# Decode value pages issued from ScalarE's DMA queue, two behind each of its key copies, in one step of a hybrid decoder layer

## The chip, the cores and the metric

The kernel runs on one core of a Trainium2 chip. The metric is the device time of one launch in microseconds (us). TensorE, VectorE, ScalarE and GpSimd (PE, DVE, ACT, POOL in the profile) compute; SyncE (SP) issues most DMAs. DMAs can be issued from SyncE, ScalarE and GpSimd.

## The reference

One inference step of a one-layer trunk, for a prompt of 512 tokens and for 8 sequences that decode 4 tokens each over a past of 2048 tokens. The decode side, cut to what matters here (page_table has 16 pages of 128 tokens per sequence):

```python
kv_past = cache_kv[page_table, l]                      # 8 sequences x 16 pages x 128 rows x (k, v) x 10 heads x 64
k_all = jnp.concatenate([kv_past[:, :, 0, ...], k_new], axis=1)
v_all = jnp.concatenate([kv_past[:, :, 1, ...], v_new], axis=1)
o_sb  = stick_breaking_attention(q_sb, k_sb_all, v_sb_all, q_pos, k_pos)      # 4 heads
o_fox = forgetting_attention(q_fox, k_fox_all, v_fox_all, cum_q, cum, q_pos, k_pos)  # 6 heads
# three dilated groups (2 heads each) over window buffers cache_dil1..3
# then: gated merge, output projection, norm, top-2 of 16 experts, norm
```

Everything is float32. Each page holds for keys, and again for values, 128 rows of 640 floats (320 KB).

## The kernel before

It runs in stages: modulation and input projection, prompt attention, the decode loop, gated merge and output projection, routing and experts, final norm. The order on each engine is written out by hand, with semaphores between the engines; there is no scheduler.

The decode loop goes over 8 sequences. On TensorE, `read_keys` does one sequence: it turns (transposes) 16 key pages and two groups of window tiles, `turn_keys(i, b0, p)` for p = 0 to 17, five transposes a page (L1032). After pages 5, 9, 13 and at the end it scores four pages at once (`score_keys`), and after pages 7, 11, 15 and at the end it turns the score rows (`turn_scores`, L1069). Between the pages it also works on the sequence before: `column_max`, `sticks`, `sums`, and from page 13 on `weigh_values`, which multiplies the 16 value pages of the previous sequence in six steps, each of which raises `v_used`. So the values of a sequence are needed about one sequence later than its keys. The first sequence runs with nothing to weigh.

Turned key pages lie in two PSUM banks, by the parity of the page. `keys_out` copies them to `kT5`: even pages on VectorE, odd pages on ScalarE (L653). A page can be turned once the page two before it has been copied out; the copies of a group of four wait for the scores of the group before. The fifth tile of each page goes to a third bank, which VectorE copies once per four pages (L1976); page 4 and so on wait for that. ScalarE's function for a sequence is `copy_out`: for each odd p the key copy; after the copies of 5, 9 and 13 the score row copy (`rows_out`, L1495), on which `turn_scores` waits; after the copies of 1, 9 and 11 the exponentials and logarithms of the previous sequence.

Key pages land in `kring`, four slots; page p may be issued when page p - 4 has been turned (semaphore `kT_mm`). Value pages land in `vpast[0]` (in `arena`, even sequences) or `vpast[1]` (in `wring`, odd ones), 16 slots each, free when the sequence two before has been weighed. Before the change SyncE issues all of it, in `sequence(i, b0)`: key pages 0 to 3, then, except in the first sequence, value pages 0 to 11 (`early`), then key pages 4 to 15, with the three window loads (1.1 MB) behind key page 8 and one value page behind each of the key pages 12 to 15. In the first sequence a value page stands behind each key page. The page's number is read from `ptab` into a register (`value_load`) and then used as an address; an odd value page reuses the register of its key page where it can. The loops run over pairs of sequences, on SyncE (2, 3), on TensorE and ScalarE (1, 2).

## Time and profile before

| | us |
|---|---|
| time, median of 3 runs | 1674.58 (1674.17 to 1683.5) |
| span of the profiled execution | 1678.0 |
| of it the decode loop, from 561 to 957 us | 396 |
| TensorE busy (7180 matmuls) | 1355.9 |
| VectorE, ScalarE, GpSimd busy | 437.0, 361.0, 164.3 |
| waits of TensorE's page turns for a key page, in the loop | 25.8, in 14 waits |

The profile is of one execution. A line of the timeline gives start, duration, engine, line of the kernel, operation and operands; in brackets the time that the engine sat idle before it, and whose work ended that. "arena<-in_cache_kv" is a page load to the key ring or to the even value buffer, "wring<-in_cache_kv" one to the odd value buffer. PEclk is the share of TensorE's full clock that was granted. The chain of work is followed back from the last instruction: each step names what released the next; a DMA's duration there runs from its issue to its landing.

### The profile page before, as it was taken

Reading aid. Unit: us, or ns where it says so; the run is one execution under the profiler, and the core shown is the slowest. Engines: PE = TensorE matmul, PEld = TensorE weight load, DVE = VectorE, ACT = ScalarE, POOL = GpSimd, SP = SyncE. Lnnn points to the kernel's source line nnn. Section 1 sums busy time; section 2 is a strip of 40 time slices with the busy share of each in tenths; the row PEclk is TensorE's granted clock in tenths of the full one; section 3 lists DMA queues with packets and bytes.
Section 4 is the critical chain, followed back from the end, with each engine's and each line's share of the span. In section 5 each row is a group of like instructions: output and inputs, shape, how many; then the busy total and the mean of one; then the engine's idle time right before and its main releaser. Section 6 shows DMA issues by size and latency. Waiting matters only on the chain.

```text
span 1678.0 us, 20728 instructions
## 1 busy us (share of the span) xinstructions
PE 1355.9 (81%) x7180; PEld 896.7 (53%) x7180; DVE 437.0 (26%) x1205; ACT 361.0 (22%) x626; POOL 164.3 (10%) x226
## 2 busy tenths in 40 slices
PE   4699997457897578878877599999992699999956
PEld 2478785333455435545545388888771344444424
DVE  3100002454343234443444201111114111111124
ACT  2200111872222122222322100000012111111104
POOL 0000000401224000000000000000002111211100
PEclk9799998777557688999989799999996799999987
DMA  8522430395000587877786422111004899999821
GB/s 319 209 100 101 159 132 1 125 327 172 1 0 1 215 299 255 253 246 255 230 260 223 148 94 85 51 50 53 0 1 119 271 327 321 306 318 315 286 107 53
DMA packets 143862, 284.74 MB, mean 170 GB/s; under 512 B 15870, under 2 KB 66759, under 8 KB 142864
## 3 DMA queue, kind: packets, MB, share of 16 engines
q1 hardware_dynamic: 133888, 260.04, 46.8%
q0 software_dynamic: 9280, 21.59, 3.6%
q10 hardware_dynamic: 624, 2.23, 0.3%
q8 instruction: 37, 0.61, 0.2%
q14 instruction: 33, 0.27, 0.0%
HBM read 270.68 MB, written 43.24 MB: 187 GB/s over the span
## 4 chain that ended last, share of the span: by engine, by line
PE 66%; DMA 8%; issue 6%; ACT 6%; DVE 6%; SPq 4%; POOL 2%; another core or an unknown queue 1%; DVEq 0%; POOLq 0%; ACTq 0%
PE psum L764 59%; PE psum L1032 3%; DMA arena<-in_cache_kv 3%; ACT L1345 3%; DMA wring<-in_w_mod 2%; SPq L499 2%; PE psum L962 2%; SPq L495 2%; POOL wring L688 2%; DVE arena L1609 1%; ACT wring L1345 1%; ACT hT L1345 1%; DVE arena L2151 1%; DMA arena<-expert_out_rows 1%; PE psum L1069 1%
## 5 line engine op out<-in xcount | busy, mean ns | idle before, releaser
L764 PE MATMUL psum<-hT,wring 128*128 128x272 f32 x1536 | 361.2, 396 | 9.7 <-ACT hT L1345 9.7
L764 PEld LDWEIGHTS psum<-hT,wring 128*128 128x128 f32 x1536 | 294.6, 192 | 74.0 <-issue 13.6
L764 PE MATMUL psum<-arena 128*8 128x128 f32 (+6 forms) x1488 | 252.2, 372 | 15.1 <-DVE arena L1609 12.6
L764 PE MATMUL psum<-wring,arena 128*8 128x128 f32 (+3 forms) x1232 | 234.5, 460 | 31.4 <-DVE arena L2151 16.6
L764 PEld LDWEIGHTS psum<-arena 128*8 128x8 f32 (+5 forms) x1488 | 133.2, 136 | 109.2 <-issue 83.8
L764 PEld LDWEIGHTS psum<-wring,arena 128*8 128x8 f32 (+3 forms) x1232 | 99.6, 130 | 141.1 <-issue 126.1
L1032 PE MATMUL psum<-small,arena 128*128 128x128 f32 x712 | 118.1, 315 | 48.9 <-DMA arena<-in_cache_kv 25.8
L764 PE MATMUL psum<-arena,wring 128*32 128x512 f32 (+1 forms) x640 | 137.6, 569 | 2.3 <-DVE arena L1609 2.3
L1032 PEld LDWEIGHTS psum<-small,arena 128*128 128x128 f32 x712 | 91.1, 160 | 80.6 <-issue 42.1
L1345 ACT ACTIVATE arena<-psum 128x544 f32<-128x544 f32 (+1 forms) x48 | 24.2, 503 | 401.7 <-PE psum L764 401.7
L1609 DVE TENSOR_TENSOR arena<-arena,psum 128x544 f32<-128x544 f32 (+8 forms) x79 | 32.2, 431 | 217.1 <-ACT arena L1345 201.7
L764 PEld LDWEIGHTS psum<-arena,wring 128*32 128x32 f32 (+1 forms) x640 | 63.5, 147 | 46.4 <-issue 36.6
L653 ACT COPY arena<-psum 128x512 f32<-128x512 f32 x64 | 37.3, 583 | 210.5 <-PE psum L1032 98.0
L653 DVE COPY arena<-psum 128x512 f32<-128x512 f32 x64 | 44.3, 692 | 137.6 <-PE psum L764 76.7
L1345 ACT ACT_TABLE_LOAD x61 | 78.3, 1283 | 1.9 <-PEq L2229 0.9
L764 PE MATMUL psum<-arena,small 128*128 128x256 f32 (+8 forms) x142 | 39.1, 402 | 34.9 <-DVE arena L1609 29.7
L688 POOL TENSOR_SCALAR wring<-wring,arena 128x384 f32<-128x384 f32 (+6 forms) x32 | 45.6, 1425 | 184.0 <-DVE arena L1824 184.0
L1650 DVE TENSOR_REDUCE modT<-psum 128x36 f32<-128x144 f32 (+1 forms) x12 | 3.7, 308 | 218.4 <-PE psum L803 218.4
L1617 DVE SCALAR_TENSOR_TENSOR arena<-psum,arena 128x256 f32<-128x256 f32 x24 | 11.6, 484 | 187.9 <-ACT arena L1345 187.9
L764 PEld LDWEIGHTS psum<-arena,small 128*128 128x128 f32 (+2 forms) x142 | 25.9, 218 | 57.4 <-issue 30.2
L764 PE MATMUL psum<-oT,arena 128*128 128x272 f32 x192 | 49.9, 404 | 6.8 <-DMA wring<-in_w_in 6.8
L1264 PE MATMUL psum<-small,arena 128*128 128x128 f32 x192 | 25.8, 279 | 34.0 <-DMA arena<-expert_in_rows,arena 34.0
(223 smaller groups left out, 1108.1 us busy)
## 6 DMA issues: line engine op xcount, KB each, us to landing
arena<-in_cache_kv SPq DMA_DIRECT2D x192, 320.0 KB, 3.7
wring<-in_w SPq DMA_DIRECT2D x48, 1024.0 KB, 11.3
wring<-in_w_mod SPq DMA_DIRECT2D x12, 2048.0 KB, 11.9
wring<-in_w_in SPq DMA_DIRECT2D x12, 2048.0 KB, 11.5
arena<-in_w SPq DMA_DIRECT2D x24, 1024.0 KB, 5.1
wring<-in_cache_kv SPq DMA_DIRECT2D x64, 320.0 KB, 4.1
out_dil_sample<-in_cache_dil SPq DMA_DIRECT2D x8, 2044.0 KB, 37.6
arena<-in_cache_dil SPq DMA_DIRECT2D x16, 512.0 KB, 5.5
```

The lines of the kernel that those rows point to most:

```text
L495: ids[p] = sp.value_load(ptab[0:1, bass.ds(b * PAGES + p, 1)], min_val=0, max_val=159)
L499: sp.dma_start(dst, pg[:, :, kv].rearrange("o k h d -> k (o h d)")).then_inc(sem(done), 16)
L653: copy(kT5[:, 0:4, c:c + 128], src.rearrange("p (j n) -> p j n", j=4)).then_inc(sem("kT_evA" if p % 2 else "kT_evD"), 1)
L688: nc.gpsimd.tensor_scalar(s, s, rowst[:, 3, n % 3:n % 3 + 1], None, ALU.mult).then_inc(sem("nrm"), 1)
L764: return T.matmul(out, lhsT, rhs, start=start, stop=stop, **k)
L962: last = T.transpose(banks[2 + tg % 2][:, 128 * (b - b0):128 * (b - b0) + 128], sc_sb[:, n % 3, 128 * b:128 * b + 128], ident)
L1032: last = T.transpose(d, a, ident)
L1069: last = T.transpose(banks[5][:, 128 * b:128 * b + 128], src[:, 128 * b:128 * b + 128], ident)
L1264: last = T.transpose(banks[k // 4][:, 128 * (k % 4):128 * (k % 4) + 128], xrow[:, slot, 128 * k:128 * k + 128], ident)
L1345: return A.activation(out, in_, fn, **k)
L1609: return V.tensor_tensor(out, a, b, op)
L2151: V.tensor_copy(xg[:, slot, 512:1024], banks[1]).then_inc(sem("xg_evD"), 1)
```

## The change

SyncE no longer issues value pages in the decode loop. ScalarE issues them in `copy_out`, pages p - 1 and p right behind the key copy of each odd p up to 15, into the same buffers, with the same semaphores. Before each of them, from the third sequence of its numbering on, it waits until the sequence two before has been weighed (all six steps). Each value page reads its number from `ptab` into a register of its own. SyncE keeps the key pages and the windows, whose wait for `v_used` at page 8 stays. Computation on TensorE, VectorE and GpSimd is unchanged.

```diff
-                def values(p):
-
-                    free = ((sem("v_used"), i * 2 * PV_STEPS + (PV_STEPS * (b0 - 2) + min(p // 2, PV_STEPS - 1) + 1)),) \
-                        if b0 >= 2 and p % 2 == 0 else ()
-                    page(p, 1, vpast[par][:, p, :], f"ld_v{par}", free)
...
-                early = 12 if b0 else 0
                 for p in range(PAGES):
...
                     if p == 8 and b0 >= 2:
-
-                        free += ((sem("v_used"), i * 2 * PV_STEPS + PV_STEPS * (b0 - 1)),)
+                        sp.wait_ge(sem("v_used"), i * 2 * PV_STEPS + PV_STEPS * (b0 - 1))
                     page(p, 0, kring[:, p % 4, :], f"ld_k{p % 4}", free)
-                    if p == 3:
-                        for v in range(early):
-                            values(v)
                     if p == 8:
                         windows()
-                    if p >= early:
-                        values(p)
...
+            def values(i, b0, p):
+
+                par = b0 % 2
+                if b0 >= 2:
+                    act.wait_ge(sem("v_used"), i * 2 * PV_STEPS + PV_STEPS * (b0 - 1))
+                page = act.value_load(ptab[0:1, bass.ds((i * 2 + b0) * PAGES + p, 1)], min_val=0, max_val=159)
+                rows = I["cache_kv"][bass.ds(page, 1), 0][:, :, 1].rearrange("o k h d -> k (o h d)")
+                act.dma_start(vpast[par][:, p, :], rows).then_inc(sem(f"ld_v{par}"), 16)
+
             def copy_out(i, b0, before):
                 steps = {1: (stick_logs,), 9: (softmax_weights,), 11: (stick_weights,)} if before else {}
                 for p in range(1, 18, 2):
                     keys_out(act, i, b0, p, A.copy)
+                    if p < PAGES:
+                        values(i, b0, p - 1)
+                        values(i, b0, p)
                     if p in (5, 9, 13):
                         rows_out(i, b0, (p - 5) // 4)
```

SyncE, in the loop, an even sequence: key page 3 and what follows it. Before, value pages 0 and 1 come next (ISA is a register or wait instruction, TENSOR_LOAD the load of a page number):

```order
L499 ISA [waits kT_mm]
L499 DMA arena<-in_cache_kv 128x640
L495 TENSOR_LOAD ptab
L495 ISA x2
L498 ISA
L499 ISA [waits v_used]
L499 DMA arena<-in_cache_kv 128x640
L499 ISA
L499 DMA arena<-in_cache_kv 128x640
L495 TENSOR_LOAD ptab
```

The same place after the change: key page 3, then key page 4, which waits only for page 0 to be turned:

```order
L499 ISA [waits kT_mm]
L499 DMA arena<-in_cache_kv 128x640
L495 ISA
L495 TENSOR_LOAD ptab
L495 ISA x2
L498 REGISTER_ALU
L499 ISA [waits kT_mm]
L499 DMA arena<-in_cache_kv 128x640
```

Twelve value DMAs and their register loads have gone from between these two key pages.

ScalarE, in the loop, an odd sequence: the key copy of page 5, the score row copy, and the wait of the next key copy, before:

```order
L649 REGISTER_ALU [waits kT_mm]
L653 COPY arena<-psum 128x4x128 [waits qk_mm]
L1492 ISA [waits qk_mm]
L1495 COPY wring<-psum 128x512 [waits sT_mm]
L647 REGISTER_ALU
L653 COPY arena<-psum 128x4x128 [waits qk_mm,kT_mm]
```

The same place after; between the two copies stand the issues of value pages 4 and 5 (line numbers shifted by the edit):

```order
L636 REGISTER_ALU [waits kT_mm]
L640 COPY arena<-psum 128x4x128 [waits qk_mm]
L1489 ISA
L1489 TENSOR_LOAD ptab
L1489 ISA x2
L1491 ISA
L1491 DMA wring<-in_cache_kv 128x640
L1489 ISA
L1489 TENSOR_LOAD ptab
L1489 ISA x2
L1491 ISA
L1491 DMA wring<-in_cache_kv 128x640
L1479 ISA [waits qk_mm]
L1482 COPY wring<-psum 128x512 [waits sT_mm]
```

Two page number loads and two DMA issues now stand ahead of the score row copy.

## Rows read from the trace of the kernel before

**Rows 1.** Busy time by sequence: stretch length, engines, clock, DMA share, GB/s; sequences 0, 1, 2, 4, 6.
```profile
564.50:606.70 42.20, 29.60 (x161) 16.76 (x162) 10.61 (x26) 8.30 (x15) 0.00 (x0) 0.77 0.94 333
606.70:655.20 48.50, 37.76 (x375) 23.93 (x374) 18.40 (x57) 12.77 (x23) 3.44 (x5) 0.89 0.84 275
655.20:700.00 44.80, 36.79 (x376) 23.88 (x375) 18.92 (x60) 12.77 (x23) 3.43 (x5) 0.92 0.83 262
...
745.80:795.20 49.40, 37.01 (x376) 23.09 (x375) 18.90 (x60) 12.77 (x23) 3.44 (x5) 0.90 0.80 259
...
840.00:888.00 48.00, 37.24 (x375) 23.74 (x375) 19.10 (x60) 12.77 (x23) 3.43 (x5) 0.89 0.85 268
```

**Rows 2.** Waits in the decode loop: us in total, times, longest.
```profile
PE psum L1032 <- DMA arena<-in_cache_kv: 25.8, 14, 5.4
```

**Rows 3.** Chain of work, sequence 4: start us, us, what.
```profile
740.21 0.33 SPq L499
...
741.39 0.33 SPq L499
...
750.26 3.46 DMA arena<-in_cache_kv
...
757.96 6.74 DMA arena<-in_cache_kv
```

**Rows 4.** TensorE's timeline, sequence 4: start us, us, what, idle before in brackets.
```profile
753.76 2.40 PE L1032 MATMUL psum<-small,arena 128*128 128x128 f32 x10 [2.60 <-DMA arena<-in_cache_kv]
...
764.83 1.30 PE L1032 MATMUL psum<-small,arena 128*128 128x128 f32 x5 [1.79 <-DMA arena<-in_cache_kv]
```

**Rows 5.** TensorE's timeline, sequence 2.
```profile
661.65 1.97 PE L1032 MATMUL psum<-small,arena 128*128 128x128 f32 x10 [1.08 <-DVE arena L1976]
...
668.90 0.60 PE L1069 MATMUL psum<-small,wring 128*128 128x128 f32 x4
...
671.10 0.74 PE L1032 MATMUL psum<-small,arena 128*128 128x128 f32 x5 [0.42 <-DMA arena<-in_cache_kv]
...
678.11 0.60 PE L1069 MATMUL psum<-small,wring 128*128 128x128 f32 x4
```

**Rows 6.** Chain of work, sequence 2.
```profile
665.80 5.16 DMA arena<-in_cache_kv
```

**Rows 7.** TensorE's timeline, sequence 0.
```profile
585.12 1.30 PE L1032 MATMUL psum<-small,arena 128*128 128x128 f32 x5 [2.99 <-DMA arena<-in_cache_kv]
...
592.01 0.60 PE L1069 MATMUL psum<-small,wring 128*128 128x128 f32 x4
```

**Rows 8.** Busy time before page 9 of sequence 3, behind it in sequence 4.
```profile
715.70:717.00 1.30, 0.00 (x0) 0.00 (x0) 0.00 (x0) 0.00 (x0) 0.00 (x0) 1.00 1.01 374
717.00:720.50 3.50, 2.57 (x15) 0.91 (x15) 0.80 (x2) 0.80 (x2) 0.00 (x0) 1.00 0.91 286
764.60:767.90 3.30, 3.07 (x14) 1.45 (x15) 0.00 (x0) 0.00 (x0) 0.00 (x0) 0.50 0.78 253
```

**Rows 9.** ScalarE's timeline, sequences 0 and 2.
```profile
590.58 0.59 ACT L1495 COPY wring<-psum 128x512 f32<-128x512 f32 x1
...
666.52 0.58 ACT L653 COPY arena<-psum 128x512 f32<-128x512 f32 x1 [5.65 <-PE psum L764]
667.00 0.59 ACT L1495 COPY wring<-psum 128x512 f32<-128x512 f32 x1
...
674.23 0.59 ACT L1495 COPY wring<-psum 128x512 f32<-128x512 f32 x1
```

**Rows 10.** DMA queues, expert stage: packets, MB, share; 1346:1347.5, then 1338:1340 us.
```profile
q0 software_dynamic: 116, 0.42, 69.5%
q1 hardware_dynamic: 165, 0.20, 36.7%
...
q1 hardware_dynamic: 685, 0.70, 109.3%
```

## The prediction

> **What bounds the kernel now.** I read the page's busy shares first, then the busy time by sequence of the decode loop, the waits inside it, the chain of work, and last the timelines of TensorE and ScalarE over single sequences. The loop runs from 561 to 957 us of a 1678.0 us span, eight sequences of 42.2 to 49.4 us each, and TensorE works 37 to 38 us of each of the later ones shown [rows 1]. It is the engine that sets the pace, in the order turn a key page, score, turn scores, weigh the previous sequence. Key pages cost it waiting time: 25.8 us in 14 waits [rows 2]. The reader should see that the sequences are of two kinds. Sequence 2 took 44.8 us; sequences 1, 4 and 6 took 48.5, 49.4 and 48.0 [rows 1].
>
> Sequence 4 shows why. SyncE issues the twelve early value pages 1.18 us apart, and only behind the last of them key page 4, at 750.26; TensorE, which had turned page 0 long before, waits 2.60 us for it, until 753.76 [rows 3, 4]. Without that hold the same spot costs 1.08 us, for a VectorE copy, as in sequence 2 [rows 5]. The second spot is page 9. Its key page stands in SyncE's queue behind the three window loads, lands 5.16 us after issue in sequence 2 and 6.74 us after it in sequence 4, and TensorE waits 0.42 and 1.79 us [rows 3 to 6].
>
> **What the change does, part by part.** Profile and runs differ: the profiled span is 1678.0, the median of the runs 1674.6. I make the sum on the span and take 3.4 off at the end.
>
> (1) Values leave SyncE. Key page 4 is then issued as soon as page 0 has been turned. Sequences 1, 4 and 6 become like sequence 2: 48.5 + 49.4 + 48.0 - 3 x 44.8 = 11.5 us less [rows 1]. The least this can be is the wait alone, three times 2.60 - 1.08, 4.5 us; the rest of 11.5 is the TensorE clock, which fell to half in the long waits. I take 11.5, since whole sequences without the hold are there to compare.
>
> (2) Sequence 0. Nine value pages, 2.9 MB, stand in SyncE's queue ahead of key page 9, and TensorE waits 2.99 us for it, until 585.12 [rows 7]. At 374 GB/s [rows 8] 2.9 MB are 7.9 us. The gain is then limited by TensorE's own work before page 9, most of whose first pages also wait for keys; by hand it can be there some 5.1 us earlier, at least 3.0. Part (3) gives back 1.7 of that. I take 3.4 (1.3 to 5.1).
>
> (3) ScalarE gets 16 issues per sequence, two behind each odd key copy. It has no id to reuse, so each is a register load and a DMA, for which the nearest row is SyncE's 1.18 us from one early value page to the next [rows 3]: 2.4 us a pair, on ScalarE's sequencer, while its copy of 0.58 us runs. What is queued behind: the score row copy, then the next key copy. After page 5 the copy starts at 666.52 and the score row copy at 667.00 [rows 9]; it would start at 668.9 and end at 669.5. TensorE turns those scores at 668.90 [rows 5], so it starts 0.7 us late, and page 8 behind it 0.3 us late; then comes page 9, which waits for its key anyway, so nothing of it shows. After page 9 the row copy moves from 674.23 to 676.1 and ends at 676.7, before TensorE wants it at 678.11 [rows 5, 9]. So in sequences 1 to 7 the issues cost nothing as long as a pair stays under about 2.9 us; above that each us of a pair is lost about twice per sequence. Sequence 0 has no weighing to cover them: the row copy at 590.58 moves to 592.5, ends at 593.1, and TensorE wanted to turn at 592.01 [rows 7, 9]: 0.9 us, and about as much once more, the 1.7 above. The wait for v_used in front of each value is already met when page 1 is turned: TensorE did the last weighing before it.
>
> (4) Values now travel while keys are awaited. Before, no value was in flight when key page 9 was; now pages 4 and 5 are issued at about 667.3 and 668.5, between the issue of key page 9 (665.80) and its landing (670.96) [rows 6, 9]. A page is 0.33 MB, at 374 GB/s 0.88 us [rows 8]. What two queues do to each other is seen in the expert stage: SyncE's queue moved 0.70 MB in 2 us alone, and 0.20 MB in 1.5 us while POOL's queue moved 0.42 MB [rows 10], that is 350 against 133 GB/s. So values are not served behind the keys but beside them. Bounds: nothing, if the second queue only fills holes; 2.0 us if both pages and a rest of pages 2 and 3 go first. I take 1.4 us later, for sequences 1 to 7: 9.8 us. The Trainium skill, "DMA: Bandwidth & Descriptors", section "Issuing engines are not separate DMA queues", says that DMAs of all issuing engines share the 16 DMA engines and interleave, and that a second issuer only saves sequencer time. By that rule alone the change would win no bandwidth and the values would land among the keys; the rows of the expert stage agree.
>
> (5) The clock. TensorE then idles about 1.5 us before page 9. In sequence 4 it idled 1.79 us and ran at half clock from there (0.50); after an idle 1.30 us in sequence 3 it stayed at 1.00 [rows 4, 8]. At half clock a page takes 1.30 against 0.74 us, and the 3.07 us of TensorE's work in that stretch would have been 1.7: 1.3 us more [rows 4, 5, 8]. I count it for three of seven sequences, 3.9 us (0 to 9.3).
>
> Sum: 1678.0 - 11.5 - 3.4 + 9.8 + 3.9 = 1676.8 on the span, less 3.4 is **1673 us** for the median. Two effects of about 15 us each cancel.
>
> **Rivals.** (B) *The values fill holes only.* Key page 9 lands as before, no clock falls: 1678.0 - 14.9 - 3.4 = 1660. For it: over the whole of sequences 1, 2, 4 and 6 the DMA engines moved 259 to 275 GB/s, below 374 [rows 1, 8]. Against it: the stretch before page 9 is the fullest of all. 0.2. (C) *Key page 9 is late by the full 2.0 us and the clock falls in each of seven sequences*: 14.0 + 9.3 instead of 13.7, so 1683, slower than before. It decides once TensorE's idle time before page 9 passes 1.8 us in every sequence. For it: queues served in turn [rows 10]. 0.18. (D) *ScalarE becomes the bound.* If its register load waits for the copy ahead, or the two issuers wait for one another, a pair may cost 4 us: turning scores late by 1.3, page 13 by 1.2 in each of seven sequences, three times 1.6 in sequence 0, 23 us more, 1696. Decides at a pair above 2.9 us. The trace has no register load on ScalarE, so only SyncE's price speaks against it. 0.1. That the hold isn't taken away is excluded by the order of SyncE's instructions.
>
> **How the numbers follow.** The forecast (effects cancel, 1667 to 1681) has 0.5; B 0.2; C 0.18; D 0.1; other 0.02. The range 1657 to 1692 takes in B and C and the near half of D. Within 1% (16.7 us, about what a measurement can tell) lie the forecast, most of C and most of B: 0.68. Faster by more needs B with more than 11.5 from part (1) or more from sequence 0: 0.14. Slower by more is D or C with dearer issues: 0.18.
>
> **What would show it.** SyncE: key page 4 issued within 0.3 us of page 0's last turn in every sequence. TensorE: waits at page 4 of about 1.1 us, on VectorE, everywhere; sequences 1, 4, 6 no longer than 2. Page 9: key landing 6 to 7 us after issue and TensorE idle 1.2 to 2 us, on a DMA; if it is 0.4, B holds. ScalarE: first to second DMA issue of a pair 1.2 us; at 2 us D holds, with TensorE's waits for ScalarE's score row copy. Sequence 0 near 39 us. The prediction is wrong if key pages other than 9 are waited for in the steady sequences, or if the half-clock stretches come elsewhere.

## The result and the profile after

The changed kernel takes 1683.41 us (median of 20 runs, 1677.31 to 1694.37) against 1675.77 us for the kernel before in the same session (20 runs, 1668.72 to 1686.44): ratio 1.0046, 95% interval 1.0028 to 1.0065. A second session gave 1683.0 against 1677.21 us, ratio 1.0024 (0.9999 to 1.0049), one of its ten executions of the changed kernel left out of the ratio because it fell in a slower state (1702.78 us). The forecast was 1673 us, a gain of 0.1%; the kernel lost 0.2 to 0.5%. The time lies in the range, within 1% of before as the forecast had it, and where rival C put it, but it moved the other way, and the balance of the forecast's terms was wrong. Each kernel was profiled twice: the spans are 1678.0 and 1673.6 us before, 1691.0 and 1682.1 us after. The rows below are of the first profile of after, an execution that took 1692.96 us, 9.6 us above the median, so they overstate the difference.

All of the difference is in the decode loop. Its busy time, for the whole loop and for sequences 0, 1, 2, 4, 5, 6, and seq 7 with the tail (columns as in [rows 1]):

```profile
563.30:977.30 414.00, 310.68 (x2985) 196.69 (x2985) 153.48 (x480) 104.70 (x185) 26.92 (x39) 0.85 0.69 240
563.30:604.90 41.60, 28.81 (x161) 16.64 (x162) 10.97 (x26) 8.31 (x15) 0.00 (x0) 0.85 0.86 303
604.90:651.20 46.30, 37.57 (x376) 23.84 (x374) 18.39 (x57) 12.84 (x23) 3.44 (x5) 0.89 0.73 254
651.20:696.50 45.30, 35.09 (x375) 22.54 (x374) 19.01 (x60) 12.85 (x23) 3.43 (x5) 0.96 0.74 260
...
743.10:794.30 51.20, 36.82 (x375) 23.96 (x374) 20.23 (x68) 12.97 (x23) 3.43 (x5) 0.90 0.66 229
794.30:845.50 51.20, 40.57 (x374) 25.78 (x375) 18.24 (x52) 12.96 (x23) 3.44 (x5) 0.84 0.68 230
845.50:896.20 50.70, 38.95 (x375) 24.33 (x376) 19.18 (x60) 12.97 (x23) 3.43 (x5) 0.87 0.67 232
896.20:977.40 81.20, 55.44 (x587) 35.79 (x586) 28.28 (x97) 18.83 (x32) 6.32 (x9) 0.73 0.58 199
```

The same query over the loop of the kernel before, first profile:

```profile
564.50:963.50 399.00, 300.67 (x2984) 191.39 (x2984) 151.66 (x480) 103.56 (x185) 26.94 (x39) 0.88 0.76 248
```

TensorE runs the same matmuls and is busy 10 us longer (310.68 against 300.67), and its mean granted share of the clock fell from 0.88 to 0.85. In the clock's records TensorE spent 120.4 us of the loop at the lower level (1.2 of 2.4 GHz), against 95.2 us before. Its waits moved. TensorE's waits in the loop (us in total, times, longest):

```profile
PE psum L1019 <- DMA arena<-in_cache_kv: 20.0, 9, 5.3
PE psum L1056 <- ACT wring L1482: 16.3, 18, 1.7
...
PE psum L1019 <- issue: 4.7, 2, 3.9
```

The waits for key pages are fewer than in [rows 2], 9 against 14, but they sit at another place. TensorE's timeline before and after page 9 of sequence 5:

```profile
800.84 2.66 PE L1019 MATMUL psum<-small,arena 128*128 128x128 f32 x10 [1.08 <-DVE arena L1975]
...
808.99 0.63 PE L1056 MATMUL psum<-small,wring 128*128 128x128 f32 x4 [0.65 <-ACT wring L1482]
809.46 0.71 PE L1019 MATMUL psum<-small,arena 128*128 128x128 f32 x5
813.14 0.74 PE L1019 MATMUL psum<-small,arena 128*128 128x128 f32 x5 [2.98 <-DMA arena<-in_cache_kv]
813.80 3.01 PE L751 MATMUL psum<-arena,wring 128*32 128x512 f32 x10
818.44 3.19 PE L751 MATMUL psum<-arena,small 128*128 128x256 f32 x6 [1.63 <-DVE arena L1608]
821.57 2.40 PE L1019 MATMUL psum<-small,arena 128*128 128x128 f32 x10
```

Page 4 is no longer held: its wait is the 1.08 us for VectorE that [rows 5] has in sequence 2. Page 9 is held for 2.98 us, where [rows 4, 5] have 1.79 and 0.42. Stretches of the same profile, the wait of sequence 5 first, and then the three at half clock that begin late in the waits at page 9 of sequences 5, 6 and 7, or just behind:

```profile
811.00:814.46 3.46, 1.32 (x13) 0.80 (x14) 0.00 (x0) 0.00 (x0) 0.00 (x0) 1.00 1.02 403
814.46:824.70 10.24, 8.61 (x26) 4.70 (x21) 2.79 (x7) 3.81 (x7) 0.00 (x0) 0.50 0.55 174
862.25:869.07 6.82, 4.85 (x15) 1.49 (x15) 0.12 (x1) 0.12 (x1) 0.00 (x0) 0.50 0.76 288
913.45:927.10 13.65, 11.19 (x35) 6.03 (x36) 2.79 (x7) 3.81 (x7) 0.00 (x0) 0.50 0.58 194
```

While TensorE waits, the DMA engines are full (403 GB/s). Right behind it they move 174 GB/s, and TensorE works at half clock for 10.24, 6.82 and 13.65 us, where [rows 8] showed a stretch of 3.3 us behind the wait of sequence 4. Behind the waits of sequences 2 and 4 (1.08 and 1.85 us) there is no such stretch. At page 4 there is one of 3.4 or 6.8 us in each of sequences 1 to 7, in both kernels and all four profiles, although the wait there is 1.08 us in most of them. The bytes that stood in front of key page 9 would have had room a few us later. They also had room earlier: at the end of sequence 4 the queues show, after and then before,

```profile
DMA packets 35, 0.06 MB, mean 7 GB/s; under 512 B 28, under 2 KB 28, under 8 KB 32
```

```profile
DMA packets 1270, 2.86 MB, mean 308 GB/s; under 512 B 153, under 2 KB 153, under 8 KB 1270
```

(786.0 to 794.3 us of after, 786.0 to 795.3 us of before). Before, value pages filled the end of the sequence; after, the DMA engines are nearly idle there.

### The profile page after: what moved, and what is told of

Its sections match the earlier page's. It is cut to its first block, busy times and chain, and to the rows that moved or that the text cites. A ratio compares the mean times of both kernels' runs of the same rounds, so it can differ in the third digit from the quotient of the medians.

```text
span 1691.0 us, 20932 instructions
## 1 busy us (share of the span) xinstructions
PE 1364.5 (81%) x7180; PEld 900.2 (53%) x7180; DVE 438.3 (26%) x1205; ACT 362.2 (21%) x627; POOL 164.4 (10%) x226
## 3 DMA queue, kind: packets, MB, share of 16 engines
q1 hardware_dynamic: 115456, 218.09, 38.4%
## 4 chain that ended last, share of the span: by engine, by line
PE 70%; DMA 6%; DVE 6%; ACT 6%; issue 6%; POOL 2%; another core or an unknown queue 2%; ACTq 1%; SPq 1%; DVEq 0%; POOLq 0%
PE psum L751 60%; PE psum L1019 4%; ACT L1332 2%; DMA wring<-in_w_mod 2%; PE psum L1056 2%; POOL wring L675 1%; PE psum L949 1%; DMA arena<-in_cache_kv 1%; DVE arena L1608 1%; ACT hT L1332 1%; DVE arena L2150 1%; DMA arena<-expert_out_rows 1%; ACT wring L1332 1%; ACTq L1491 1%
## 5 line engine op out<-in xcount | busy, mean ns | idle before, releaser
L751 PEld LDWEIGHTS psum<-hT,wring 128*128 128x128 f32 x1536 | 293.0, 191 | 74.1 <-issue 13.7
L751 PE MATMUL psum<-arena 128*8 128x128 f32 (+6 forms) x1488 | 251.8, 371 | 13.2 <-DVE arena L1608 10.8
L751 PE MATMUL psum<-arena,wring 128*32 128x512 f32 (+1 forms) x640 | 141.3, 582 | 2.3 <-DVE arena L1608 2.3
L751 PE MATMUL psum<-arena,small 128*128 128x256 f32 (+8 forms) x142 | 43.6, 438 | 35.8 <-DVE arena L1608 30.5
## 6 DMA issues: line engine op xcount, KB each, us to landing
wring<-in_w SPq DMA_DIRECT2D x48, 1024.0 KB, 11.5
```

Source lines behind the costliest of these rows:

```text
L751: return T.matmul(out, lhsT, rhs, start=start, stop=stop, **k)
```

## The experiments

Two theories. K: the value bytes beside the keys make key page 9 late, and the waits lower the clock. I: the issues on ScalarE's own order cost the time, by what stands behind them.

**Which of the two.** In the first, the score row copy goes ahead of the value issues, in the second a value load brings a tenth of its bytes, in the third SyncE issues all, at nearly the same points (12 to 15 together behind key page 15). With a tenth of the bytes the rest of the value buffer isn't loaded, and the weighing multiplies old data there.

```diff
 # a1_rows_first, in copy_out
                     keys_out(act, i, b0, p, A.copy)
+                    if p in (5, 9, 13):
+                        rows_out(i, b0, (p - 5) // 4)
                     if p < PAGES:
                         values(i, b0, p - 1)
                         values(i, b0, p)
-                    if p in (5, 9, 13):
-                        rows_out(i, b0, (p - 5) // 4)
 # a2_tenth, in values
-                rows = I["cache_kv"][bass.ds(page, 1), 0][:, :, 1].rearrange("o k h d -> k (o h d)")
-                act.dma_start(vpast[par][:, p, :], rows).then_inc(sem(f"ld_v{par}"), 16)
+                rows = I["cache_kv"][bass.ds(page, 1), 0][:, :, 1, 0:1].rearrange("o k h d -> k (o h d)")
+                act.dma_start(vpast[par][:, p, 0:64], rows).then_inc(sem(f"ld_v{par}"), 16)
 # a3_one_queue, in sequence (SyncE); ScalarE's issues are taken out
+                    if p >= 5 and p % 2:
+                        for v in (p - 5, p - 4):
+                            values(v)
+                for v in range(12, PAGES):
+                    values(v)
```

> The changed kernel with one thing moved: after the key copies of pages 5, 9 and 13 ScalarE makes the score row copy first and issues the two value pages behind it. Changed kernel against before: 1.0046, 1683 to 1676 us. Theory K (value bytes travel beside the keys and delay key page 9, and TensorE's clock falls in the wait): page 9 hardly moves, since the values are issued only 0.5 us later, so 1679 to 1683, ratio 1.002 to 1.0045, key page 9 still landing 5.5 to 8 us after its issue. Theory I (the issues on ScalarE's sequencer are what costs): TensorE's waits for the score row copy go from 16.3 us back to the 10.7 us of before, and the clock with them, so 1672 to 1677, ratio under 1.001.

> The changed kernel, but each value page load brings only the first of ten heads, a tenth of the bytes, with the same number of issues, register loads and semaphores; the rest of the value buffer is not loaded, so the weighing multiplies old data there. Theory K: key page 9 lands 5 to 6 us after its issue as before the change, TensorE waits 0.4 us or less for it, sequences 1 to 6 take about 45 us each, total 1661 to 1669, ratio 0.991 to 0.996. Theory I: unchanged, 1680 to 1686, with sequences of 45 to 51 us.

> The values are paced as in the changed kernel, but issued by SyncE: two pages behind each of the key pages 5, 7, 9, 11, 13, four more behind 15; no hold before key page 4, nothing on ScalarE. One queue, so values 4 and 5 stand behind key page 9, values 0 to 3 ahead of it. Theory K in the form that the second queue matters (served in turn): key page 9 lands 5.5 to 6.5 us after issue instead of 5.4 to 8.5, total 1665 to 1673, ratio 0.994 to 0.998. Theory K in the form that only the bytes matter, whatever the queue: 1672 to 1680. Theory I: 1668 to 1675, as ScalarE has none of it, with key page 9 as late as in the changed kernel.

Measured: 1682.34 us (ratio 1.0037, 1.0012 to 1.0062), 1669.63 us (0.9958, 0.9937 to 0.9978) and 1689.9 us (1.0083, 1.0061 to 1.0106). TensorE's waits in the loop, first in the one with the rows first, then with a tenth, then with one queue:

```profile
PE psum L1019 <- DMA arena<-in_cache_kv: 23.5, 12, 5.2
...
PE psum L1056 <- ACT wring L1482: 10.7, 8, 1.7
```

```profile
PE psum L1056 <- ACT wring L1482: 16.7, 18, 1.7
...
PE psum L1019 <- DMA arena<-in_cache_kv: 8.4, 6, 5.4
```

```profile
PE psum L1028 <- DMA arena<-in_cache_kv: 28.2, 13, 5.4
...
PE psum L1065 <- ACT wring L1491: 10.7, 8, 1.7
```

The first lies in the range that theory K had given, the second 0.6 us above it, the third above every range. The waits for the row copy cost next to nothing: without them (10.7 us as before) the time hardly moved; page 9 waited 1.95 us instead of 1.79 (means of sequences 1 to 7). With all issues in place and a tenth of the bytes, the loss is gone (the profiled execution took 1659.25 us, 10 us below the median of that run). With the bytes at nearly the same points and no issue on ScalarE, it is there and larger. So it is the bytes and their place, and not ScalarE's issues.

The run with one queue is no clean test of the second queue. Values stand ahead of key page 9 in SyncE's own queue there, so that it is issued 3.0 us behind page 5's turns instead of 1.8; it then lands 6.3 us after issue, against 5.8 before the change and 7.0 after it (means of sequences 1 to 7). With one queue the key page waits its turn longer, with two its load takes longer.

**The windows.** The window loads stand ahead of key page 9; here they go behind key page 11 (`if p == 8:` becomes `if p == 11:`, with the wait in front), in the changed kernel and in the kernel before.

> The changed kernel with the three window loads (1.1 MB) behind key page 11 instead of 8. They are needed from page 16 on. Theory K: nothing but two key pages and values is in flight when key page 9 is, it lands within 5 us, no wait for a DMA at page 9, total 1667 to 1674, ratio 0.995 to 0.999. Theory I: 1679 to 1684. If the windows then come late for page 16 (under 10 us from issue to use), TensorE waits there instead, and the total stays above 1676.

> The kernel before with the windows behind key page 11 instead of 8. In the changed kernel this moved TensorE's wait from page 9 to page 12 (2 to 5 us each) and cost 1.6% more. Theory K: here no values travel between pages 4 and 11, so key page 9 comes in time (8 us of waits at page 9 gone), and key page 12 stands behind 1.1 MB with 5 us in hand, against 6 needed: waits of 0 to 2 us at page 12. Total 1670 to 1682, ratio 0.996 to 1.003, much less than the 1.6% of the changed kernel. If the place of the windows alone made those 1.6%, values or not: 1700 or more.

Measured: 1711.11 us (1.0208, 1.0185 to 1.0231) and 1678.73 us (1.0011, 0.9991 to 1.0031). In the first the wait moved to page 12 in every sequence, 1.6 to 4.6 us, and the waits for key pages grew to 36.2 us in 17; in the second page 12 was waited for in sequences 0 and 7 (4.7 and 0.9 us), the waits of page 9 went away and nothing was gained. The first number is far above both theories' ranges for it, the second is in its range. Windows behind key 11 collide with the changed kernel's values. How much of the lateness of key page 9 they make in the changed kernel is not settled by this, since moving them only moved the collision.

**When the values go, if SyncE issues them.** The kernel before with eight early value pages instead of twelve, the others behind keys 10 to 15; then the kernel before with ScalarE issuing half of the twelve early ones (0 to 5 on SyncE, 6 to 11 at the end of ScalarE's `copy_out`); then the same with the windows ahead of key 4.

```diff
 # b2_early8, in sequence
-                early = 12 if b0 else 0
+                early = 8 if b0 else 0
...
-                    if p >= early:
+                    if b0 == 0:
                         values(p)
+                    elif p >= 10:
+                        for v in LATE[p]:
+                            values(v)
 # LATE = {10: (8,), 11: (9,), 12: (10,), 13: (11, 12), 14: (13,), 15: (14, 15)}
```

> The kernel before, SyncE alone: eight early value pages instead of twelve, the other eight behind key pages 10 to 15 (one each behind 10, 11, 12 and 14, two behind 13 and 15). The hold before key page 4 shrinks by 4.7 us and so goes, page 9 is left alone, ScalarE issues nothing. Theory K: 1663 to 1670, ratio 0.992 to 0.997, unless key pages 13 to 15 (1 to 4 us early before) come late behind the values. If TensorE waits for key page 15 in most sequences, 1670 to 1678.

> The kernel before, but of the twelve early value pages SyncE issues six (0 to 5) and ScalarE the other six (6 to 11) at the end of copy_out of the sequence before, where it idles 7 us; pages 12 to 15 stay with SyncE. So the hold before key page 4 goes and no value is moved into the stretch before page 9. Theory K: sequences 1, 4 and 6 fall from 48.5, 49.4, 48.0 to about 45 us, the others stay, total 1663 to 1668, ratio 0.992 to 0.996. Theory I (a value issue on ScalarE costs wherever it stands) or no gain from the hold at all: 1674 to 1680.

> b1_split, and from sequence 1 on the windows are issued behind early value page 5, once the sequence two before has been weighed, so ahead of key page 4 and in the quiet stretch. Theory K: key page 9 then lands 3 to 4 us after its issue, no wait at page 9, another 4 to 9 us less than b1_split, 1655 to 1662, ratio 0.987 to 0.992. Against it: 1.1 MB now lies ahead of key page 4; if that lands more than 5 us after its issue TensorE waits at page 4 instead and the total is that of b1_split or above.

Measured: 1667.49 us (0.9952, 0.9929 to 0.9975), and a second time 1669.41 us (0.994, 0.992 to 0.9959); the split 1676.27 us (1.0002, 0.9981 to 1.0023); with windows early 1687.13 us (1.0059, 1.0038 to 1.008). The first is in theory K's range; the two splits are above theirs by 8 and by 25 us. In the first variant sequences 1, 4 and 6 take 45.0, 44.7 and 44.5 us, sum 134.2 against 145.9 before; in the second profiles it is 134.9 against 140.4. The mean of the two, 8.6 us, is what taking the hold away is worth, and about what the whole kernel gains (9.0 and 8.7 us). What the split did to key page 4 stands in its chain of work in sequence 4:

```profile
749.84 0.03 SPq L499
749.87 0.03 issue
749.90 6.44 DMA arena<-in_cache_kv
```

The hold in SyncE's queue is gone, and the same value pages, from the other queue, make the load last 6.44 us instead of the 3.46 of [rows 3]. Over sequences 1 to 7 it is 5.1 us on the mean, against 3.1 in the variant with eight early pages, so only two of the seven waits at page 4 are for the key page (2.64 and 1.48 us). In sequence 1 of both splits TensorE also waits 3.7 us at page 3 for ScalarE's key copy, behind the issues at the end of `copy_out`. With the windows early, page 9 is waited for in sequence 0 alone, but page 4 waits 2.3 to 3.7 us for its key page in five sequences.

**The same places, from ScalarE.** The value pages of that variant at its times, but in ScalarE's order: 0 to 7 behind the last row copies of the sequence before, 8 to 15 behind the key copies of pages 11, 13 and 15.

> The value pages at the times of the variant with eight early pages, but issued from ScalarE's queue: pages 0 to 7 at the end of the sequence before, 8 and 9, 10 to 12, 13 to 15 behind the key copies of pages 11, 13 and 15. Theory K (only the time of the bytes matters): close to that variant's 1667 plus 0 to 5 us for the issues on ScalarE, whose waits by TensorE grow to 15 us or so: 1665 to 1674. Theory I: the issues stand in ScalarE's order whenever they are made, so it stays near the changed kernel, 1678 to 1690.

Measured 1689.49 us (1.0077, 1.0054 to 1.01), about 21 us above the variant. Theory K's number missed, theory I's range (1678 to 1690) holds. ScalarE's timeline of the turn from sequence 2 to 3:

```profile
694.31 0.58 ACT L1497 COPY wring<-psum 128x512 f32<-128x512 f32 x1 [1.92 <-PE psum L766]
695.16 6.46 ACTq L1506 DMA_DIRECT2D wring<-in_cache_kv  x6
707.32 0.58 ACT L655 COPY arena<-psum 128x512 f32<-128x512 f32 x1 [12.42 <-issue]
```

Six issues (6.46 us, and the wait for free slots ahead of some) keep ScalarE from its next key copy until 707.32, and TensorE's page 3 waits 4.49 us for that copy at 707.96, in sequences 1, 3 and 5 (3.4, 4.5 and 3.3 us). That is 11.2 us of the 21. Key page 4 also landed later, 5.6 us after issue (mean of sequences 1 to 7) against 3.1. So theory I holds for this place: who issues matters where a wait or a row of issues stands ahead of a copy that TensorE needs. In the change itself, with two issues at a time, it showed in sequence 0 alone (part (2) below).

**Sequence 0.** The variant with eight early pages, its sequence 0 with values only behind keys 10 to 15.

> The variant with eight early value pages on SP, and in sequence 0 the value pages only behind keys 10 to 15 (two each, the last four behind key 15) instead of one behind each key. Sequence 0 took 41.7 us in that variant against 38.0 us with a tenth of the value bytes. Theory K: sequence 0 falls by 1.5 to 3.5 us, and the kernel comes to about 1664 (ratio 0.993). If the pages come too late for sequence 0's own products, sequence 1 grows by as much.

Measured 1663.98 us (0.9929, 0.9903 to 0.9956), the lowest median of all, though its interval and the variant's overlap. Sequence 0 went from 41.7 to 38.4 us, and sequence 1 grew from 45.0 to 47.3.

**Work put into the wait.** Ten small matmuls behind page 8's turns, in the changed kernel and in the kernel before.

```diff
                     turn_keys(i, b0, p)
+                    if p == 8:
+                        for _ in range(10):
+                            mm(banks[6][:, 448:512], ident, ident[:, 0:64])
```

> The changed kernel with ten more small matmuls (identity by 64 columns, into columns of a psum bank that nothing reads) behind key page 8's turns on TensorE, in every sequence: work that keeps the engine busy in the wait for key page 9, about 1.4 us at full clock, 2.8 us at half. It computes nothing that is used. Theory K (the value bytes ahead of key page 9 make the wait, and most of the loss is the lower clock behind it): the wait shrinks, the time at half clock in the loop falls from 120 us to 90 or less, and the kernel comes out at 1668 to 1680, under the changed kernel although TensorE has more to do. If the clock is no part of the loss, the filler is hidden in waits or adds up to 1.4 us a sequence: 1683 to 1694. Theory I (the issues on ScalarE's sequencer cost the time) expects no gain either: 1683 to 1694.

> The same ten small matmuls in the kernel before, as a control. There page 9 was waited for in sequences 0, 2 and 4 alone; the filler costs 1.4 us where nothing is waited for. Expected by both theories: within 10 us of the kernel before, 1668 to 1686 (ratio 0.995 to 1.006); if it gains as much as the filler gains in the changed kernel, then the filler's gain is not tied to the value pages.

Measured: 1693.02 us (1.0099, 1.0079 to 1.0119) and 1692.21 us (1.0101, 1.0082 to 1.0119). The control missed its range: the filler costs 16 us in the kernel before, 2 us a sequence. In the changed kernel it costs 9.6 us, and 1693 is in the range that was given to theory I and to a loss in which the clock has no part (1683 to 1694), not in theory K's; the time at half clock fell from 120.4 to 100.9 us, not to 90. As the filler alone costs more than was thought, this decides little. With the spot before page 9 filled in both, the two kernels are level within 1 us. That speaks for the change's loss being at this spot, but says nothing for the clock: the filler covers the wait itself as well.

**The wait alone.** Therefore an idle was made by hand, in the variant with eight early pages, with no transfer moved: GpSimd does two or six additions from the end of page 8's turns on, and TensorE's page 9 waits for them; in a control GpSimd does six and TensorE doesn't wait.

```diff
 # GpSimd, at the head of each sequence's part (six additions)
+                    pool.wait_ge(sem("kT_mm"), i * 36 + 18 * par + 9)
+                    for _ in range(5):
+                        link(nc.gpsimd.tensor_tensor(holdb, ident, ident, ALU.add))
+                    nc.gpsimd.tensor_tensor(holdb, ident, ident, ALU.add).then_inc(sem("pv_mm"), 1)
 # TensorE, ahead of turn_keys(i, b0, p)
+                    if p == 9:
+                        pe.wait_ge(sem("pv_mm"), i * 2 + b0 + (NU + 1))
```

> The variant with eight early value pages on SP (1667 us), with a wait made by hand: from the end of key page 8's turns GpSimd does two additions of 128x128 (0.73 us were measured for one of 128x256 in this loop, so some 0.4 us each by its size), and TensorE's page 9 waits for the second. No transfer is moved. An idle of about 1 us before page 9 in each of eight sequences. If idle time is lost once and no more: at most 8 us, 1667 to 1676, with TensorE's busy time in the loop as in the variant. If an idle of that size makes the clock fall (as is thought of waits of 1.8 us and more): the same, since 1 us is under it.

> The same with six additions, an idle of about 2.6 us before page 9 in each of eight sequences, as long as the changed kernel's waits in its last three sequences (2.6 to 3.1 us). If idle time is lost once and no more: at most 8 times 2.6 = 21 us, 1688, and TensorE's busy time in the loop as in the variant with eight early pages. If such waits bring the half clock (the theory under test, the rest of theory K): the loop's time at half clock rises from 71.6 us by 3.4 to 7 us a sequence, 27 to 55 us, TensorE's busy time by 0.4 of that, 11 to 22 us, and the kernel comes to 1695 to 1710.

> Control: the six additions on GpSimd as in the long hold, but TensorE doesn't wait for them. Expected by both theories: as the variant with eight early value pages, 1664 to 1671. More than that is what GpSimd's work itself costs VectorE or the others, and is to be taken off the two others.

Measured: short 1671.46 us (0.9966, 0.9949 to 0.9982), long 1702.4 us (1.0166, 1.0136 to 1.0196), control 1669.49 us (0.9964, 0.9947 to 0.9981). Against the control, the short idle, 1.0 us in each of six sequences by the timeline (in the two others a key page came later than it), costs 2.0 us in all; their ratios can't be told apart. The long one costs 32.9 us. The long hold's waits, its loop and one stretch of it:

```profile
PE psum L1041 <- POOL wring L707: 23.3, 8, 2.9
```

```profile
561.80:981.90 420.10, 312.33 (x2985) 193.51 (x2985) 151.57 (x480) 103.56 (x185) 46.62 (x88) 0.85 0.72 235
622.10:635.80 13.70, 11.08 (x35) 6.00 (x35) 2.74 (x7) 3.71 (x7) 0.80 (x2) 0.50 0.50 165
```

and the control's loop:

```profile
565.40:957.50 392.10, 300.96 (x2984) 192.97 (x2984) 151.92 (x480) 103.56 (x185) 46.63 (x88) 0.87 0.76 252
```

Eight waits of 2.9 us, 23.3 us in all, made TensorE's busy time 11.4 us longer (312.33 against 300.96) and the kernel 32.9 us slower: 1.4 times the idle put in. The control itself waited 5.9 us at page 9 for key pages, so the idle added is 17.4 us, and each us of it cost 1.9. The half-clock stretch of 13.70 us begins in the hold of sequence 1 and runs on behind it (page 9 starts at 623.10), with no transfer moved. Behind the eight equal holds the half-clock stretches are 3.4, 13.7, 0, 6.8, 3.4, 0, 13.7 and 6.8 us long (sequences 0 to 7). So it is shown that waits of some 3 us before page 9 cost more than their length, and that the clock falls behind most of them, for up to as long as in the changed kernel; a single wait does not tell how long. A wait of 1 us there costs next to nothing.

**Second profiles.**

> The changed kernel once more, for a second profile beside the first, whose span (1691.0 us) was 7.6 us above its median. If the long stretches at half clock behind page 9 (6.8 to 13.7 us each in sequences 5 to 7) belong to the kernel, they come again in other sequences and the half-clock time in the loop is again above 110 us, against 95.2 us in the kernel before. If they were that execution's own, the half-clock time falls to the kernel before's.

> The kernel before once more, for a second profile: what TensorE's time at half clock (95.2 us) and its busy time (300.7 us) in the decode loop do from one execution to the next. Ratio 1.000 by construction. If the clock carries the change's loss, half clock stays under 102 us, the lower of the changed kernel's two profiles (120.4 and 101.9), and busy under 308.

> The variant with eight early value pages once more, for a second profile (the first had 71.6 us at half clock, the control of the long hold, almost the same kernel, 98.6). If 71.6 belongs to the variant, it comes again within 10 us; if it was that execution's, some 85 to 95 us. Time 1664 to 1671 by either.

The loop of the changed kernel, of the kernel before and of the variant with eight early pages, each in its second profile:

```profile
561.10:966.80 405.70, 308.04 (x2985) 194.61 (x2985) 153.39 (x480) 104.60 (x185) 26.97 (x39) 0.87 0.70 244
```

```profile
562.90:959.40 396.50, 297.05 (x2984) 188.60 (x2985) 151.93 (x480) 103.56 (x185) 26.92 (x39) 0.89 0.76 249
```

```profile
565.80:954.70 388.90, 293.92 (x2985) 186.30 (x2985) 151.75 (x480) 103.61 (x185) 26.98 (x39) 0.90 0.77 254
```

The kernel before, run once more, took 1677.38 against 1678.08 us (ratio 1.0008, 0.9984 to 1.0032). Time at half clock in the loop: 101.9 us (120.4 in the first profile), 89.3 (95.2) and 78.2 (71.6). The changed kernel missed the 110 us that its expectation asked for, yet is above both others. Its long stretches came again in other sequences: page 9 waited 4.55 us in sequence 1 and 3.35 us in sequence 2, with 3.4 us at half clock from the end of the former on, and 6.8 us that begin 1.8 us before the end of the latter. Busy time is the steadier sign: 310.7 and 308.0 us after, 300.7 and 297.1 before, 292.6 and 293.9 in the variant. The control of the long hold, nearly that variant, had 98.6 us and 301.0, so a single profile can be off by some 8 us of busy time.

**The clock of all executions.** The granted clock of every execution is on record, for the whole kernel; 2 x (1 - clock) x span is its time at half clock:

| | executions | mean clock | us at half clock, mean |
|---|---|---|---|
| before, five sessions | 118 | 0.8765 | 414.0 |
| after, both sessions | 29 | 0.8762 | 416.3 |
| eight early pages, both sessions | 21 | 0.8790 | 403.5 |
| long hold | 5 | 0.8672 | 451.9 |
| its control | 12 | 0.8776 | 408.6 |

One execution scatters by 12 us, so the first difference is 2.3 us with an interval of some 5 us either way. The profiles had 12 us more at half clock over the whole kernel and 19 in the loop. They are not typical: over all executions the changed kernel has hardly more time at half clock than the kernel before. Against the variant with eight early pages it has 12.8 us more, and the long hold has 43 us more than its control.

## Why the prediction was wrong

The terms against the means of the two profiles of each kernel, in the loop:

| | forecast, us | measured, us |
|---|---|---|
| waits at page 4, sequences 1 to 7 | -4.5 | -5.1 |
| waits at page 9, sequences 1 to 7 | +9.8 | +7.2 |
| sequence 0 | -3.4 | -0.7 |
| TensorE's clock: given back in part (1), lost in part (5) | -7.0 + 3.9 = -3.1 | +10.5 (about +1 by all executions) |
| loop | -1.2 | +12.1 |

The page 4 row is 7 x (1.06 - 1.79), the page 9 row 7 x (1.79 - 0.76), from the mean waits in the timelines; the clock row is TensorE's busy time, 309.4 less 298.9; sequence 0 is (41.6 + 40.7 - 42.2 - 41.5) / 2 and holds a little of the clock. The loop's 12.1 us also hold 1.9 us (the mean of 3.9 and nothing) of the idle at TensorE's jump that the last section shows. The spans differ by 10.8 us, the medians by 5.8 and 7.6, so the profiles overstate the loss. The estimate by all executions takes their 2.3 us more at half clock, and 0.4 us of TensorE's time for each: +1 us, between -1 and +3. The factor is from the profiles: 18.1 us of busy time for 48.8 us at half clock between the variant with eight early pages and the changed kernel, 19.7 for 51.4 between that variant and the long hold. With +1 in that row the measured terms add up to 2.4 us, so 3 to 5 us of the loss stay without a term.

**Part (1), the hold: right in its mechanism, too large in its clock.** Key page 4 is issued 0.15 us after page 0's last turn (795.80 against 795.65), and page 4 waits 0.96 to 1.09 us on VectorE in sequences 1 to 7. The 11.5 us are too much: the variant with eight early pages gains 8.6 us in sequences 1, 4 and 6, as the mean of two profiles. The prediction put 7.0 of the 11.5 down to the clock. Its own rows speak against that: in [rows 1] TensorE is busy 37.76 + 37.01 + 37.24 = 112.0 us in the three sequences, only 1.6 us more than 3 x 36.79. The clock's records of the first profile of before have 6.8 us at half clock at page 4 in each of the three and 3.4 us in sequence 2, so three times 3.4 us, about 4 us of time, were to be had; all executions of the variant say the same (10.5 us less at half clock). And the stretch of 3.4 us does not go with the hold: it stayed at page 4 in every sequence.

**Part (2), sequence 0: too much.** 0.7 us instead of 3.4. Key page 9 came earlier (TensorE turned it at 582.43 instead of 585.12, which is 19.1 instead of 20.6 us after the sequence's start), but page 5 now waited 2.06 us for ScalarE's key copy, which stands behind two issues, and 1.88 us in the second profile. These two issues, the first that ScalarE makes, took 3.78 us from start to end, where later pairs took 1.4 to 1.9. The step counted the row copies behind the issues and not the next key copy.

**Part (3), ScalarE's issues: right in sequences 1 to 7.** From the end of a key copy to the row copy behind its pair of issues (columns of the timeline as before):

```profile
828.02 0.58 ACT L640 COPY arena<-psum 128x512 f32<-128x512 f32 x1 [1.28 <-PE psum L751]
828.79 1.48 ACTq L1491 DMA_DIRECT2D wring<-in_cache_kv  x2
830.38 0.58 ACT L1482 COPY wring<-psum 128x512 f32<-128x512 f32 x1 [1.77 <-issue]
```

Copy to row copy 2.36 us, forecast 2.4, first to second issue 1.14. TensorE's waits for row copies rose by 5.6 us, and as said they don't show: with them taken away the kernel took 1682.3 us, against 1683.4 and 1683.0. Rival D is out.

**Part (4), values beside the keys: right, a little large.** Key page 9 landed 5.7 us after issue before (5.74 and 5.78, means of sequences 1 to 7), 6.9 and 7.1 after: 1.2 us later, where 1.4 was taken. A second queue is not needed for the loss: the same bytes from one queue cost more (1689.9), by a key page 9 that is issued later. But the loads of the two queues do lengthen each other, as the argument from [rows 10] had it: 7.0 us for key page 9 with two queues against 6.3 with one. By the Trainium skill, "DMA: Bandwidth & Descriptors", section "Issuing engines are not separate DMA queues", the DMAs of all issuing engines run on the same 16 DMA engines and interleave. Key page 4's load agrees, which took 5.1 us beside the other queue's values in the split and 3.1 us in the variant with eight early pages (means of sequences 1 to 7).

**Parts (1) and (5), the clock: the step that failed.** The forecast had the clock give back 7.0 us behind page 4 and take 3.9 behind page 9, a net gain of 3.1. Measured is a net loss: 10.5 us in the two profiles of each kernel, about 1 us by all executions. The gain was too large, as said. The loss in part (5) was counted as 1.3 us for each of three waits, from the 3.3 us at half clock of sequence 4. Against the variant with eight early pages, which issues no value page between key pages 4 and 10 outside sequence 0, all executions give 12.8 us more at half clock, about 5 us of time. So the sum was near, but its picture was not. First, the length: a stretch at such a wait lasted nothing to 13.7 us, for waits of equal length too, as the long hold shows. One row was taken as the size of all. Second, the average: waits of 1.5 us were expected in each sequence. They came as 0.0, 1.08, 0.0, 1.85, 2.98, 3.10 and 2.56 in one profile, 4.55, 3.35, 1.38, 0.0, 1.42, 1.96 and 0.84 in the other. The means, 1.7 and 1.9, were near the 1.5 expected, but waits of 1 us at this place are free and those of 2.9 us cost 1.4 times their length, so the spread is what is paid. With the clock, part (2) failed by 2.7 us.

Rival C gave the right time, 1683, but not by its own sum. It wanted an idle above 1.8 us in every sequence and 14.0 us of waits with 9.3 of clock on top of the full gain of 14.9; the waits were uneven, they came to 7.2, and the gain was smaller. Its mechanism, a late key page 9 and the clock behind it, is there. That its number fits is luck in part.

**What stays open.** That the value bytes make the loss, by way of longer waits at page 9, is shown by the run with a tenth of the bytes and by the landing times. How the loss divides into wait and clock is not: the profiles have most of it in the clock, all executions hardly any of it, and 3 to 5 us are not accounted for. In the profiles the time at half clock goes with the long waits: the long hold has 18.7 us more in waits above 1.8 us than its control and 24.5 us more at half clock, the changed kernel 14.5 us and 19 us more than the kernel before (means). Why a wait of 1 us is followed by half clock at page 4 and not at page 9 was not tried.

## What to carry to other kernels

Look where the DMA engines are idle as well as where they are full: taking loads out of one queue's way paid here only where the bytes went into a stretch with room. Eight early pages at the end of each sequence and the rest behind key 10 gave 0.5%, all of them in the middle lost 0.2 to 0.5%. Price a stall of TensorE by its length and its clock: before page 9 an idle of 1 us was free, one of 2.9 us cost 4.1. Don't read the clock from one profile or two, when the granted clock of every execution is on record. Don't put a row of issues, or a wait, into the order of an engine whose copies the pace-setter needs.

## What the runs showed of the hardware that was not expected

At the jump back of TensorE's loop, before sequence 5, the changed kernel's first profile has an idle that no semaphore ends:

```profile
789.91 0.51 PE L751 MATMUL psum<-small,wring 128*128 128x8 f32 x4
794.31 2.90 PE L1019 MATMUL psum<-small,arena 128*128 128x128 f32 x12 [3.89 <-issue]
```

and in the DMA queues of that stretch two packets of instructions:

```profile
q8 instruction: 2, 0.03, 2.3%
```

It came at the head of sequence 5 in the two splits too (5.34 and 6.84 us), in the short hold and in the control of the long one (3.9 and 3.8), at sequences 3 and 5 in both filled kernels (3.2 to 3.9), and never at the odd heads in the two profiles of the kernel before. That TensorE waits there for its instructions is a guess from the packets' time. In one profile of the changed kernel it was 3.9 us of the loop, in the other nothing.
